# A split running sum for the stick-breaking attention, and a later place for its low half

## The reference

```
z        = q.k * scale + bias                      (one row per query, one column per key)
log_rest = where(key < query, log_sigmoid(-z), 0)  # = -softplus(z)
after    = reverse cumsum(log_rest) - log_rest     # all keys after this one, up to the query
a        = where(key < query, exp(log_sigmoid(z) + after), 0)
out      = a @ v
```

## Time and profile before

| | us |
|---|---|
| median of 3 runs | 1932.49 |
| lowest and highest | 1931.7, 1933.04 |
| the profiled execution | 1931.59 |
| its span, first to last instruction | 1929.9 |

### The profile page before, as it was taken

The page is one execution under the profiler, slowest core; times in us unless marked ns, Lnnn a source line. Parts: engine busy times, 40 slices in busy tenths (PEclk is TensorE's granted clock), DMA queues, the critical chain, the costliest instruction groups (busy, mean ns, idle before and its releaser), DMA issues.

```text
span 1929.9 us, 28935 instructions
## 1 busy us (share of the span) xinstructions
PE 1873.4 (97%) x11137; PEld 1751.9 (91%) x11137; DVE 832.3 (43%) x1064; ACT 542.7 (28%) x871; POOL 294.2 (15%) x319
## 2 busy tenths in 40 slices
PE   6999999999999999999999989999999999999997
PEld 6778786968869989999999969999999999999996
DVE  5565747375612222223224286443124442344436
ACT  5464647372110010000002453222012220123213
POOL 1121213132401101101110121001000101001012
PEclk9999999999799999999999999999999999999998
DMA  5202020304231111111114122111111111111302
GB/s 161 67 23 65 18 70 0 87 0 127 81 98 49 44 39 49 43 49 44 44 49 143 34 88 70 51 43 44 45 53 43 43 43 44 55 43 43 135 29 93
DMA packets 162139, 113.45 MB, mean 59 GB/s; under 512 B 5374, under 2 KB 152198, under 8 KB 161805
## 3 DMA queue, kind: packets, MB, share of 16 engines
q1 hardware_dynamic: 160893, 108.08, 18.7%
q10 hardware_dynamic: 1200, 4.75, 0.7%
HBM read 95.60 MB, written 13.40 MB: 56 GB/s over the span
## 4 chain that ended last, share of the span: by engine, by line
PE 84%; DVE 8%; issue 3%; ACT 2%; POOL 2%; DMA 1%; SPq 0%; DVEq 0%; POOLq 0%; ACTq 0%
PE ps L1415 64%; PE ps L1425 10%; DVE zl L1098 2%; PE misc L1506 2%; POOL sp_hi L590 2%; PE misc L1401 1%; PE ps L1680 1%; PE ps L1496 1%; PE misc L1588 1%; PE misc L1587 1%; DVE later L1115 1%; DVE later L1111 1%; DVE sp_lo L1120 1%; PE ps L1491 1%; DVE hn L1272 0%
## 5 line engine op out<-in xcount | busy, mean ns | idle before, releaser
L1020 DVE TENSOR_TENSOR w_lo<-stage,w_hi 128x1024 fp32r<-128x1024 f32 x148 | 184.6, 1247 | 591.4 <-POOL w_hi L546 591.1
L1415 PE MATMUL ps<-h_hi,w_lo 128*128 128x344 f32 x1896 | 404.4, 322 | 0.7 <-DVE y_lo L1211 0.7
L1415 PE MATMUL ps<-h_lo,w_hi 128*128 128x344 f32 x1896 | 403.1, 321 | 0.0
L1415 PE MATMUL ps<-h_hi,w_hi 128*128 128x344 f32 x1896 | 401.0, 320 | 0.0
L546 POOL TENSOR_SCALAR w_hi<-stage 128x1024 fp32r<-128x1024 f32 x148 | 157.5, 1064 | 1291.8 <-PE ps L1415 1103.9
L1415 PEld LDWEIGHTS ps<-h_hi,w_lo 128*128 128x128 f32 x1896 | 319.6, 188 | 2.7 <-issue 1.4
L1415 PEld LDWEIGHTS ps<-h_lo,w_hi 128*128 128x128 f32 x1896 | 321.4, 189 | 0.0
L1415 PEld LDWEIGHTS ps<-h_hi,w_hi 128*128 128x128 f32 x1896 | 316.4, 188 | 0.0
L1425 PE MATMUL ps<-h_hi,w_lo 128*128 128x344 f32 x408 | 150.7, 369 | 0.0
L943 ACT ACTIVATE up<-ps 128x1032 f32<-128x1032 f32 x44 | 45.5, 1034 | 354.7 <-PE ps L1415 353.0
L1425 PE MATMUL ps<-h_hi,w_hi 128*128 128x344 f32 x408 | 137.0, 336 | 0.0
(11 more groups left out here) (258 smaller groups left out, 2586.9 us busy)
## 6 DMA issues: line engine op xcount, KB each, us to landing
stage<-in_w_in SPq DMA_DIRECT2D x48, 512.0 KB, 3.9
stage<-in_w_up SPq DMA_DIRECT2D x44, 512.0 KB, 3.8
stage<-in_w_down SPq DMA_DIRECT2D x16, 448.0 KB, 3.3
stage<-in_w_branch SPq DMA_DIRECT2D x24, 256.0 KB, 2.7
x_scratch<-trunk SPq DMA_DIRECT2D x1, 4128.0 KB, 12.5
x_back<-x_scratch SPq DMA_DIRECT2D x1, 4128.0 KB, 14.4
x_tok<-in_x_prompt SPq DMA_DIRECT2D x8, 512.0 KB, 8.2
kv_pg<-in_cache_k SPq DMA_DIRECT2D x16, 256.0 KB, 3.6
```

What stands on the lines that cost most here:

```text
L1020: V.tensor_tensor(w_lo[par][:, :, :], stage[par][:, :, :], w_hi[par][:, :, :].bitcast(F32), ALU.subtract).then_inc(w_lo_made, 1)
L1415: last = M(ps[par][:, c, :], w[par][:, k, :], x[:, c * CH:(c + 1) * CH], start=(k == 0 and s == 0), stop=(k == n - 1 and s == 2))
```

## The change

`later` and the split of the chunk's own softplus are replaced by one running sum. `sums` holds, for each query, the softplus of this chunk's keys plus that of the later chunks' keys on the same partition. It is made for every chunk, the last too. For the columns where there is a chunk before, it is one instruction of three inputs, and for new columns one with a tile of ones as the second tensor. GpSimd makes the high half from `sums`, when the whole sum is there, and VectorE the low half by a plain subtraction. Both halves have four buffers in place of three.

TensorE takes `neg_tri` times this chunk's halves, and in place of the one float32 product with `neg_ones` two fp32r products with `neg_rest` (minus one on the partitions before this key's) times the halves of the chunk before. Since own and later blocks share one sum per partition, `neg_tri` now brings the later blocks of the partitions from this key's on with it, and `neg_rest` adds those of the partitions before.

VectorE's order in a chunk becomes: zl(c), the low half of c-1, the sum of c. The low half of c-1 thus stands behind zl(c) and ahead of the sum of c, and the last low half of a turn behind the loop. ScalarE's abs of c now waits for the low half of c-4 and not of c-3. The one-token attention gets one product more, since `neg_ones` is gone. The parts of the diff that only rename or count are left out:

```diff
-    later_upto = [0]
-    for n, (_, _, _, W, top, last) in enumerate(CHUNKS):
-        wider = not top and W > CHUNKS[n - 1][3]
-        later_upto.append(later_upto[-1] + (0 if last else 1 + wider))
-    NLATER = later_upto[NCK]
+    sums_upto = [0]
+    for n, (_, _, _, W, top, _) in enumerate(CHUNKS):
+        sums_upto.append(sums_upto[-1] + 1 + (not top and W > CHUNKS[n - 1][3]))
+    NSUMS = sums_upto[NCK]
...
-        neg_ones = sb("neg_ones", [P, P])
         neg_tri = sb("neg_tri", [P, P], F32R)
+        neg_rest = sb("neg_rest", [P, P], F32R)
...
-        sp_hi = [sb(f"sp_hi{i}", [P, HALF], F32R, s_att) for i in range(3)]
-        sp_lo = [sb(f"sp_lo{i}", [P, HALF], F32R, s_att) for i in range(3)]
-        later = [sb(f"later{i}", [P, HALF], F32, s_att) for i in range(4)]
+        sums = [sb(f"sums{i}", [P, HALF], F32, s_att) for i in range(2)]
+        s_hi = [sb(f"s_hi{i}", [P, HALF], F32R, s_att) for i in range(4)]
+        s_lo = [sb(f"s_lo{i}", [P, HALF], F32R, s_att) for i in range(4)]
...
-            nc.gpsimd.memset(neg_ones[:, :], -1.0).then_inc(consts, 1)
+            nc.gpsimd.memset(neg_rest[:, :].bitcast(F32), -1.0).then_inc(consts, 1)
...
-            nc.gpsimd.affine_select(out=neg_tri[:, :], in_=neg_ones[:, :], compare_op=ALU.is_ge, fill=0.0,
+            nc.gpsimd.affine_select(out=neg_tri[:, :], in_=neg_rest[:, :], compare_op=ALU.is_ge, fill=0.0,
                                     base=0, pattern=[[-1, P]], channel_multiplier=1).then_inc(consts, 1)
 
             nc.gpsimd.affine_select(out=mask_b[:, :], in_=mask_b[:, :], compare_op=ALU.is_ge, fill=0.0,
                                     base=0, pattern=[[-1, P]], channel_multiplier=1).then_inc(consts, 1)
-            pool.wait_ge(consts, NCONST + 1)
+            pool.wait_ge(consts, NCONST + 3)
+            nc.gpsimd.affine_select(out=neg_rest[:, :], in_=neg_rest[:, :], compare_op=ALU.is_ge, fill=0.0,
+                                    base=-1, pattern=[[1, P]], channel_multiplier=-1).then_inc(consts, 1)
...
-                    pool.wait_ge(spn_ready, p * NCK + (c + 1))
+                    pool.wait_ge(sums_made, p * NSUMS + sums_upto[c + 1])
                     pool.wait_ge(cum_ready, p * NCK + (c + 1))
                     pool.sem_inc(hi_begun, 1)
-                    nc.gpsimd.tensor_scalar(sp_hi[c % 3][:, 0:W], zl[c % 4][:, 0:W], bias_p[:, hh:hh + 1], 1.0,
-                                            ALU.add, ALU.mult).then_inc(hi_ready, 1)
+                    nc.gpsimd.tensor_scalar(s_hi[c % 4][:, 0:W], sums[c % 2][:, 0:W], 1.0, 0.0,
+                                            ALU.mult, ALU.add).then_inc(hi_ready, 1)
...
-                    act.wait_ge(sp_ready, p * NCK + (c + 1))
+                    if c >= 4:
+                        act.wait_ge(sp_ready, p * NCK + c)
...
-                nl = 0
+
+                def sums_lo(c):
+
+                    W = CHUNKS[c][3]
+                    dve.wait_ge(cum_ready, p * NCK + (c + 1))
+                    dve.wait_ge(hi_ready, p * NCK + (c + 1))
+                    V.tensor_tensor(s_lo[c % 4][:, 0:W], sums[c % 2][:, 0:W], s_hi[c % 4][:, 0:W].bitcast(F32),
+                                    ALU.subtract).then_inc(sp_ready, 1)
...
-                    if not last:
-                        dve.wait_ge(spn_ready, p * NCK + (c + 1))
-                        dve.wait_ge(cum_ready, p * NCK + (c + 1))
-                    if top:
-                        V.tensor_scalar(later[c % 4][:, 0:W], t, bias_p[:, hh:hh + 1], None, ALU.add
-                                        ).then_inc(later_ready, 1)
-                        nl += 1
-                    elif not last:
-                        Wb = CHUNKS[c - 1][3]
-                        dve.wait_ge(later_ready, p * NLATER + nl)
-                        V.scalar_tensor_tensor(later[c % 4][:, W - Wb:W], t[:, W - Wb:W], bias_p[:, hh:hh + 1],
-                                               later[(c - 1) % 4][:, 0:Wb], ALU.add, ALU.add
-                                               ).then_inc(later_ready, 1)
-                        if Wb < W:
-                            V.tensor_scalar(later[c % 4][:, 0:W - Wb], t[:, 0:W - Wb], bias_p[:, hh:hh + 1], None,
-                                            ALU.add).then_inc(later_ready, 1)
-                            nl += 1
-                        nl += 1
-                    dve.wait_ge(hi_ready, p * NCK + (c + 1))
-                    V.scalar_tensor_tensor(sp_lo[c % 3][:, 0:W], t, bias_p[:, hh:hh + 1],
-                                                sp_hi[c % 3][:, 0:W].bitcast(F32), ALU.add, ALU.subtract
-                                                ).then_inc(sp_ready, 1)
-                assert nl == NLATER
+                    if c > 0:
+                        sums_lo(c - 1)
+                    dve.wait_ge(spn_ready, p * NCK + (c + 1))
+                    total = sums[c % 2]
+                    Wb = 0 if top else CHUNKS[c - 1][3]
+                    if Wb:
+                        dve.wait_ge(sums_made, p * NSUMS + sums_upto[c])
+                        V.scalar_tensor_tensor(total[:, W - Wb:W], t[:, W - Wb:W], bias_p[:, hh:hh + 1],
+                                               sums[(c - 1) % 2][:, 0:Wb], ALU.add, ALU.add).then_inc(sums_made, 1)
+                    if Wb < W:
+                        V.scalar_tensor_tensor(total[:, 0:W - Wb], t[:, 0:W - Wb], bias_p[:, hh:hh + 1],
+                                               ones[:, 0:W - Wb], ALU.add, ALU.mult).then_inc(sums_made, 1)
+                sums_lo(NCK - 1)
...
-                    M(z, neg_tri[:, :], sp_lo[c % 3][:, 0:W], start=False, stop=False, skip_group_check=True)
-                    t = M(z, neg_tri[:, :], sp_hi[c % 3][:, 0:W], start=False, stop=top, skip_group_check=True)
+                    M(z, neg_tri[:, :], s_lo[c % 4][:, 0:W], start=False, stop=False, skip_group_check=True)
+                    t = M(z, neg_tri[:, :], s_hi[c % 4][:, 0:W], start=False, stop=top, skip_group_check=True)
                     if not top:
                         Wb = CHUNKS[c - 1][3]
-                        pe.wait_ge(later_ready, p * NLATER + later_upto[c])
-                        t = M(z[:, W - Wb:W], neg_ones[:, :], later[(c - 1) % 4][:, 0:Wb], start=False, stop=True,
+                        M(z[:, W - Wb:W], neg_rest[:, :], s_lo[(c - 1) % 4][:, 0:Wb], start=False, stop=False,
+                          skip_group_check=True)
+                        t = M(z[:, W - Wb:W], neg_rest[:, :], s_hi[(c - 1) % 4][:, 0:Wb], start=False, stop=True,
...
-            M(dec_sums[:, 0:half], neg_ones[:, :], sp_d[:, half:], start=False, stop=True, skip_group_check=True
-              ).then_inc(dec_cum, 1)
+            M(dec_sums[:, 0:half], neg_tri[:, :].bitcast(F32), sp_d[:, half:], start=False, stop=False,
+              skip_group_check=True)
+            M(dec_sums[:, 0:half], neg_rest[:, :].bitcast(F32), sp_d[:, half:], start=False, stop=True,
+              skip_group_check=True).then_inc(dec_cum, 1)
```

More of the change, by code:

```diff
@@ L320, in build @@
             ktok_ps, ktok_made, vtok_ps, vtok_made, small_ps, small_made, tok_out, z_ready,
-            abs_made, e_made, l_ready, q_pads, spn_ready, hi_ready, sp_ready, later_ready, cum_ready,
+            abs_made, e_made, l_ready, q_pads, spn_ready, hi_ready, sp_ready, sums_made, cum_ready,
             att_ready, pv_done, yc_hi_made, yc_made, pad_zero, own_mask, own_made, dec_o_ps, xg_ps,
@@ L336, in build @@
             "small_ps", "small_made", "tok_out", "z_ready", "abs_made", "e_made", "l_ready", "q_pads",
-            "spn_ready", "hi_ready", "sp_ready", "later_ready", "cum_ready", "att_ready", "pv_done",
+            "spn_ready", "hi_ready", "sp_ready", "sums_made", "cum_ready", "att_ready", "pv_done",
             "yc_hi_made", "yc_made", "pad_zero", "own_mask", "own_made", "dec_o_ps", "xg_ps",
@@ L655, in _ @@
             act.dma_start(g_pre[:, :], norm_mix_pre[0, :].partition_broadcast(P)).then_inc(gpre_in, 16)
-            act.wait_ge(consts, NCONST + 4)
+            act.wait_ge(consts, NCONST + 5)
             for b in range(len(IN_BATCHES) + 1):
@@ L1170, in _ @@
             V.tensor_tensor(zf, dec_sums, zf, ALU.add).then_inc(dec_arg, 1)
-            dve.wait_ge(consts, NCONST + 4)
+            dve.wait_ge(consts, NCONST + 5)
             V.tensor_reduce(pick[:, :], ident[0:NS * H, 0:NS * H].rearrange("p (h b) -> p b h", h=H), AX_X, ALU.add
@@ L1430, in _ @@
             ys = [(y_hi[:, k, :], y_lo[:, k, :]) for k in range(BT)]
-            pe.wait_ge(consts, NCONST + 4)
+            pe.wait_ge(consts, NCONST + 5)
             FIRST_Q = {4: (0, 0, KT), 5: (0, KT, KT), 6: (0, 2 * KT, KT),
```

## The result

| | before | after |
|---|---|---|
| median, same chip (7 runs each) | 1932.72 | 1938.59 |
| lowest and highest | 1931.51, 1933.73 | 1936.94, 1941.43 |
| the profiled execution's span | 1929.9 | 1936.8 |

The ratio after/before is 1.0034, interval 1.0022 to 1.0045: slower by 5.9 us. The forecast was 3.8 us slower. The two spans are 6.9 us apart, more than the medians, because the profiled execution of the kernel before was 1.1 us faster than its median.

The account below looks back on a forecast made before the run. TensorE was taken to wait for `sp_lo` early in each head and set the pace later. Four turns x 0.9 + 0.2 = 3.8 us slower, 1935.4, median 0.9 higher: 1936.3; range 1925 to 1943, the forecast's own 1933 to 1939.

Parts of the forecast that it names:

- TensorE's step: Sums in the touched loop: two fp32r products replace a two-pass float32 one, saving 5.3 us per turn, 21.1 in all.
- The rival in which it stays two passes: TensorE's neg_rest products still take two passes, adding 21 us; chance 1%.
- GpSimd and VectorE: Full chunks: high half 0.69 us instead of 1.21, low half 0.68, overlap with zl adding 0, at most 0.5.
- L and the pace: L: 2.94 us, scores of c+2 to sums of c; P: TensorE's work meanwhile. If P is shorter, pace (L + P)/2.
- the rival of VectorE's order: Low half waits for zl's end, 0.87 us behind its start, not 0.67: 1943.9 us, half of it 1940; chance 0.23.
- The turn that it worked through: Second turn of the loop, chunk by chunk with queues in program order: ends 0.9 us later than before.
- that sign of being wrong: Forecast is wrong if TensorE hardly waits for the low half in chunks 13 to 16.
- The rest behind the loop: One-token attention gets one more 64-column float32 product in two passes, 0.2 to 0.3 us: +0.2.
- The clock: TensorE's granted clock stays 1.00 in the loop; rival of one fall per turn gives 1954 us, chance 0.05.
- the two signs by which the forecast was to be called wrong: TensorE hardly waits for the low half in chunks 13 to 16, or granted clock leaves 1.00 before 450 us.
- the trace at 548 us: Stretch of the trace before that kept its clock, taken as evidence against throttling by waits between matmuls.
- The saving gets through: Rival: TensorE's saving outweighs the new waits, 1927.5 us or less, fully hidden 1911.6; chance 0.24.

Follow-up runs that it names:

- split-at-9 kernels: First weight split of each turn moved from chunk 7 to 9: changed kernel 1927.64 us, with low halves also early at seven chunks 1924.24; kernel before 1929.44.
- the changed kernel with the strict abs wait: Changed kernel with ScalarE's abs of chunk c waiting for the low half of c-3 again, not c-4: 1948.52 us, 1.0081 of before.
- the running sum in its own turn: Changed kernel with every low half ahead of the next chunk's zl instead of behind it: 1963.75 us, 1.0162 of before.
- the deferred kernel: Kernel before with only its low half (sp_lo) of chunk c-1 moved behind zl of chunk c: 1958.66 us, 1.0133 of before.

## Why the prediction was right, and where it was off

**TensorE's step.** Right. `neg_rest` is issued once per operand, 0.23 us apart for 512 columns (191.58 and 191.81 in the trace after). The rival in which it stays two passes is out.

**GpSimd and VectorE.** Right in size: high half 0.62 for 0.69, low half 0.69 for 0.68, second part 0.35 for 0.35. Nothing was added for the overlap with zl, and nothing showed: zl is 0.74 or 0.75 long.

**L and the pace.** A full chunk of the profile after:

```profile
188.26 0.69 ACT L705 ACTIVATE zl<-ps,bias_p 128x512 f32<-128x512 f32 x1 [0.42 <-PE ps L1479]
...
188.85 0.71 ACT L715 ACTIVATE zl<-zl,ones 128x512 f32<-128x512 f32 x1
...
189.60 0.75 DVE L1107 SCALAR_TENSOR_TENSOR zl<-ps,nbias_p,zl 128x512 f32<-128x512 f32 x1 [0.51 <-ACT zl L715]
...
190.26 0.68 DVE L1076 TENSOR_TENSOR s_lo<-sums,s_hi 128x512 fp32r<-128x512 f32 x1
...
191.00 0.51 PE L1490 MATMUL ps<-s_lo,neg_tri 128*128 128x512 f32 x1 [0.23 <-DVE s_lo L1076]
```

From abs to the sums it is 2.74 us; the forecast had 2.74 for the same steps (2.94 with 0.20 ahead of abs). The 0.20 holds too: this chunk's last scores began at 187.84 and took 0.23 to issue, 0.19 before abs. The low half follows zl by 0.66, with the next chunk's zl still running: the rival of VectorE's order (0.87) is out. What the prediction made of L is less sure. Full chunks were to be 2.6 to 2.9 us apart and were 2.43 to 2.93 (5.08 at the weight split), and the run without `neg_rest` shows the waiting steps of chunks 13 to 16 paced by ScalarE, which the prediction does not name as a bound. The turn that it worked through took every queue in order and has these steps right all the same (2.43, 2.68 and 2.54 us; measured 2.46, 2.67 and 2.51).

**Chunk by chunk**, the sums from a turn's first scores in us, before, forecast (its times less 171.36) and measured in an undisturbed turn:

| chunk | before | forecast | after |
|---|---|---|---|
| 3 | 12.00 | 13.32 | 13.50 |
| 6 | 21.84 | 23.38 | 23.54 |
| 7 | 25.34 | 26.30 | 26.45 |
| 12 | 37.34 | 38.89 | 39.15 |
| 14 | 41.21 | 43.75 | 44.06 |
| 17 | 50.30 | 51.86 | 52.17 |
| 20 | 59.74 | 60.24 | 60.59 |
| 23 | 71.12 | 72.33 | 72.59 |

From chunk 3 on the forecast is 0.15 to 0.35 us early (chunks 0 to 2 agree within 0.06), and it has the deepest place (14, then 2.5 us behind; measured 2.85) and the recovery to 20 where they are. TensorE's waits were to rise from about 20 us to about 45; on the row of the weight load, which is the first to wait, they rise from 26.2 to 53.6, by 6.9 us a turn for a forecast of 6.2. In chunks 13 to 15 TensorE waits 0.19, 0.56 and 0.45 us for the low half, so that sign of being wrong did not show.

**The sizes that were off.** The turn was to be 0.9 us longer and was 1.2: 1.2 us over the loop, from the same early 0.3 us. The rest behind the loop was to cost 0.2; with the fourth turn it is 1.7, so about 0.5. Of that, 0.43 is the added product of the one-token attention (at 545.01 us, with a granted clock of 0.50), which had been priced at 0.2 to 0.3.

**The clock.** This term was wrong, and it was one of the two signs by which the forecast was to be called wrong: the granted clock left 1.00 before 450 us. I took no fall and set the price of one at 4.5 us. One came, after the 2.10 us wait at chunk 7 of the second turn, lasted 3.3 us and cost 1.6. The Trainium skill, "TensorE: Matmul & The Clock Gate", section on HAM oscillation, which I had weighed and set aside by the trace at 548 us, has groups of matmuls begin slow after waits. The trace agrees only in part: the products behind the wait ran at full rate for the first microsecond (0.22 to 0.24 us apart from 196.42 on) and slowed from about 197.1, and at the same place of the three other turns they did not slow. In the split-at-9 kernels, where that wait is gone, the loop has no fall. So 1.2 x 4 + 0.5 + 1.6 = 6.9 us, the difference of the spans. The forecast's sum was 3.8, and the three misses (1.2 in the turns, 0.3 behind the loop, 1.6 of clock) all go one way, so nothing cancelled. With the medians' difference of 5.9 the time came out 0.4 us under the upper end of the forecast's own 1933 to 1939.

**The saving gets through.** Out for this kernel, but by little. It needed some 1.5 us a turn, and one place, the weight split at chunk 7, held 2.3. I had said that the order at chunk 7 and the copies "are in the program whatever the durations are"; the first of them is what decided the sign. I had not said that the program could have it elsewhere.

**What I left out.** The abs wait at c-4 had no term. My turn was worked with the looser one, so the sum was right, but the reader was not told that 9 us hang on that line.

## What to carry to other kernels

Where two engines hand a piece back and forth, work out the cycle through each pair of them (here 3.21, 2.83 and 2.77 us), and look for an engine without a pause, before counting what a faster engine saves. TensorE's shorter step came through nearly whole where TensorE did not wait, and not at all where ScalarE was never idle. An average such as 60% can match a rule that the single steps do not follow, so check the rule step by step. After a change of order, look for the big instruction that now stands ahead of a late one. Moving one weight split by two chunks was worth 0.6% in the changed kernel and 0.13% in the kernel before, so an order tuned for one kernel must be tuned again for the next. A guard on a buffer that costs nothing before can cost nearly 0.5% after: relax it together with the change, or it hides what the change is worth.

## What the hardware showed that was not expected

- TensorE's granted clock fell inside a busy loop after a wait of 2.10 us, from 1.00 to 0.50 (2.4 to 1.2 GHz) for some 3.3 us, in the same turn of two executions and not in the three other turns with the same wait. Over the loop it fell three times in the changed kernel with the strict abs wait, twice in the running sum in its own turn, once in the deferred kernel, and in none of the other kernels' profiled executions. The length of a wait does not sort these: of the eight falls three came behind a wait of 2.10 us and one behind 1.80, but four came next to one of only 0.69 to 0.76 us, with one of 0.96 to 1.16 some two microseconds ahead of it, and four waits of 2.55 us brought none.
- GpSimd's high half takes 0.62 us with two immediates as scalars, 0.69 with a bias per partition, 1.21 beside one VectorE instruction with two SBUF inputs and 1.57 beside two (the deferred kernel, 195.34). VectorE's low half takes 1.45 for 0.69 beside GpSimd's weight split, which keeps its 1.05.
